# Expert weights loaded through two DMA queues: SyncE keeps the first, third and fifth pair, ACT takes the second, fourth and sixth

## The reference

```
for each expert e (its tokens xb):
    hgu   = xb @ w_up_gate[e] + b_up_gate[e]          # 1024 x 2048
    x_glu = min(hgu[:, :1024], 7);  x_lin = clip(hgu[:, 1024:], -7, 7)
    hact  = x_glu * sigmoid(1.702 * x_glu) * (x_lin + 1)
    y     = hact @ w_down[e] + b_down[e]              # 1024 x 1024
```

## Time and profile before

| | |
|---|---|
| median of three runs | 1576.78 us |
| profiled execution | 1576.77 us, span 1575.0 us |
| PE busy in the span | 1464.4 us (93%) |
| DVE, ACT, POOL busy | 465.3, 423.3, 458.0 us (30%, 27%, 29%) |
| SP's DMA queue (q1) | 498.71 MB, 78.7% of the 16 engines' time |
| ACT's DMA queue (q10) | 2.36 MB, 0.5% |
| mean granted PE clock | 0.981 |

### The profile page before, as it was taken

One profiled execution on the slowest core, in us unless ns is written; L12 is line 12 of the kernel. 1 busy time (PEld: TensorE's weight loads), 2 busy tenths in 40 slices (PEclk: granted clock), 3 DMA queues, 4 the chain that ended last, 5 costly groups with the idle time before them and its releaser, 6 DMA issues.

```text
span 1575.0 us, 18643 instructions
## 1 busy us (share of the span) xinstructions
PE 1464.4 (93%) x7492; PEld 828.8 (53%) x7493; DVE 465.3 (30%) x842; ACT 423.3 (27%) x564; POOL 458.0 (29%) x356
## 2 busy tenths in 40 slices
PE   8999999998898998899998898988899999999998
PEld 7887533333333333333333333333698767799986
DVE  6526411111111111111111111111557494323211
ACT  6354301101001001001001001001754775443332
POOL 6836000000000000000000000000779656689994
PEclk9999999999999999999999999999999999999999
DMA  9534899999999999999999999999655323545540
GB/s 344 203 111 148 364 427 427 429 425 428 425 427 428 427 427 427 426 427 427 427 429 426 426 426 428 426 429 402 203 176 178 129 87 132 189 134 187 188 161 27
DMA packets 93479, 502.32 MB, mean 319 GB/s; under 512 B 8091, under 2 KB 38419, under 8 KB 66643
## 3 DMA queue, kind: packets, MB, share of 16 engines
q1 hardware_dynamic: 91904, 498.71, 78.7%
q10 hardware_dynamic: 1491, 2.36, 0.5%
HBM read 500.00 MB, written 1.05 MB: 318 GB/s over the span
## 4 chain that ended last, share of the span: by engine, by line
PE 61%; DMA 26%; DVE 5%; ACT 4%; issue 2%; POOL 2%; SPq 0%; DVEq 0%; ACTq 0%
DMA ring<-in_w_up_gate 24%; PE PS L939 19%; PE PS L573 9%; PE PS L575 9%; PE PS L574 9%; PE PS L957 8%; POOL w_low L2413 2%; PE PS L900 1%; DMA ring<-in_w_ple_gate 1%; PE PS L946 1%; ACT w_high L1335 1%; DVE arena L2053 1%; DVE arena L2050 1%; DVE arena L2048 1%; ACT arena L1493 1%
## 5 line engine op out<-in xcount | busy, mean ns | idle before, releaser
L2413 POOL TENSOR_TENSOR w_low<-ring,w_high 128x512 fp32r<-128x512 f32 (+1 forms) x352 | 457.8, 1342 | 1095.8 <-ACT w_high L1335 1094.8
L939 PE MATMUL PS<-ring,arena 128*64 128x512 f32 x1792 | 408.1, 609 | 20.4 <-DMA ring<-in_w_up_gate 20.4
L939 PEld LDWEIGHTS PS<-ring,arena 128*64 128x64 f32 x1792 | 126.8, 140 | 284.3 <-issue 246.0
L957 PE MATMUL PS<-ring,arena 128*64 128x512 f32 x1024 | 238.5, 620 | 27.9 <-ACT arena L1493 27.9
L1484 ACT ACTIVATE arena<-arena 128x512 f32<-128x512 f32 x32 | 20.1, 630 | 761.6 <-DVE arena L2047 761.6
L1335 ACT ACTIVATE w_high<-ring 128x2048 fp32r<-128x2048 f32 (+1 forms) x89 | 166.3, 1880 | 112.4 <-PE PS L575 89.6
L957 PEld LDWEIGHTS PS<-ring,arena 128*64 128x64 f32 x1024 | 75.8, 142 | 168.5 <-issue 168.5
L2047 DVE TENSOR_SCALAR arena<-PS 128x512 f32<-128x512 f32 x32 | 22.1, 692 | 461.1 <-PE PS L939 461.1
L573 PE MATMUL PS<-w_high,XNT_h 128*128 128x512 f32 (+1 forms) x336 | 135.3, 403 | 3.9 <-DVE XNT_l L1763 2.2
L573 PE MATMUL PS<-XNT_h,w_high 128*128 128x256 f32 (+1 forms) x464 | 131.2, 283 | 2.2 <-DVE XNT_l L1746 1.3
L574 PE MATMUL PS<-w_low,XNT_h 128*128 128x512 f32 (+1 forms) x336 | 131.5, 391 | 0.0
(11 more groups left out here) (374 smaller groups left out, 1492.7 us busy)
## 6 DMA issues: line engine op xcount, KB each, us to landing
ring<-in_w_up_gate SPq DMA_DIRECT2D x112, 2048.0 KB, 23.0
ring<-in_w_down SPq DMA_DIRECT2D x64, 2048.0 KB, 21.4
ring<-in_w_in SPq DMA_DIRECT2D x35, 1024.0 KB, 5.5
ring<-in_w_gate_up SPq DMA_DIRECT2D x22, 1024.0 KB, 5.1
arena<-in_w_up_gate SPq DMA_DIRECT2D x16, 1024.0 KB, 20.9
cst<-in_w_up_gate SPq DMA_DIRECT2D x16, 1024.0 KB, 24.9
ring<-in_w_down SPq DMA_DIRECT2D x11, 1024.0 KB, 4.9
ring<-in_w_out SPq DMA_DIRECT2D x8, 1024.0 KB, 5.1
```

The costliest lines, as they stand in the source:

```text
L939: ins = nc.tensor.matmul(PS[64 * (n % 2):64 * (n % 2) + 64, 4 + n // 2, :], x, w[:, n * 512:(n + 1) * 512], start=False, stop=c == KC - 1, ...
L957: ins = nc.tensor.matmul(PS[64 * n:64 * n + 64, 7, :], lhs, w[:, k, n * 512:(n + 1) * 512], start=(j, k) == (0, 0), stop=(j, k) == (1, 3))
L2413: ins = nc.gpsimd.tensor_tensor(LOW[raw_slot(key)][:, at], slot(raw_slot(key))[:, at], HIGH[m % BUF][:, at].bitcast(F32), ALU.subtract)
```

## The change

The list `ON_SP` = (0, 2, 4) replaces the range of six in SP's `next_loads` and in the single expert between its two loops, so SP issues pairs 0, 2 and 4 of experts 1 to 31. Pairs 1, 3 and 5 are issued by ACT inside its expert loop: `next_pair(e, j)` waits until PE has used pair j of expert e and then issues pair j of expert e+1. The load of pair 1 stands ahead of the sigmoid, that of pair 3 behind the sigmoid and ahead of the spread copy, that of pair 5 behind the activation's copy. ACT's loop covers 31 experts, and expert 31 follows without loads. Expert 0 is still loaded by SP alone. The conditions of the waits, the slots, the sources and the sizes are as before.

```
+ON_SP = (0, 2, 4)
...
             def next_loads(i, first, early):
-                for j in range(PER_EXPERT):
+                for j in ON_SP:
...
-            for j in range(PER_EXPERT):
+            for j in ON_SP:
                 if j != TWICE:
                     sp.wait_ge(sem("w_used"), (IN_ORDER - 1) * PER_EXPERT + (before_experts + j + 1))
                     expert_load(IN_ORDER, j)
...
-            with act.Fori(0, E) as e:
+            def next_pair(e, j):
+                act.wait_ge(sem("w_used"), e * PER_EXPERT + (before_experts + j + 1))
+                src = (w_up[1:] if j < UPS else w_down_e[1:])[e]
+                rows = src[j * 256:(j + 1) * 256, :] if j < UPS else src[(j - UPS) * 512:(j - UPS + 1) * 512, :]
+                act.dma_start(slots2(EXPERT_SLOT[j]), rows.rearrange("(p k) n -> p (k n)", p=P)).then_inc(landed[EXPERT_SLOT[j]], 16)
+            def expert_copies(e, loads):
+                if loads:
+                    next_pair(e, 1)
                 sigmoid("glu", "sig", e + 1)
+                if loads:
+                    next_pair(e, 3)
                 act.wait_ge(sem("spread"), e + 1)
                 nc.scalar.activation(SPT, PS[:, 7, 0:256], ACT.Copy).then_inc(sem("sT_slots"), 1)
                 act.wait_ge(sem("hT_ps"), e + 1)
                 nc.scalar.activation(HTS, PS[:, 6, :], ACT.Copy).then_inc(sem("hT"), 1)
+                if loads:
+                    next_pair(e, 5)
+            with act.Fori(0, E - 1) as e:
+                expert_copies(e, True)
+            expert_copies(E - 1, False)
```

## The result

Over 12 runs each, the changed kernel took 1584.84 us (1579.05 to 1589.12), the kernel before 1576.88 us (1572.92 to 1578.47): a ratio of 1.0056, 95% interval 1.0047 to 1.0066. The medians differ by 8.0 us; the ratio goes by the means, which differ by 8.9. The profiled execution took 1583.52 us, 6.75 more than that of before.

A forecast was written before the change was run, and what follows sets the result against it. It took the DMA engines as the limit, 29.47 us an expert against PE's 27.20. Issues cost nothing; landing order delays the last down part 5.2 us, less 1.3 absorbed: 1576.77 plus 3.9 gives 1580.7 us, range 1570 to 1588.

The forecast's parts named there:

- if PE waits for pairs 0, 1 or 4: Sign in the profile after: PE waiting for loads of these pairs would show the prediction wrong.
- the waits at pair 3: Sign in the profile after: PE's waits on loads again at pair 3, about 2.2 us each.
- ACT's landings above 24 us: Sign in the profile after: ACT's pairs take a median above 24 us to land, its queue being at half rate.
- Where the time goes: Expert layer: DMA engines set the pace, 29.47 us an expert at 427 GB/s; PE needs 27.20, 2.27 less.
- Equal shares: DMA engines with two queues: a pair takes 9.82 us while the other queue has work, total rate as before.
- The rival of turns by whole pairs: Engines alternate queues by whole pairs, landing 4.91 us apart in the old order; 1576.8 us, nothing lost; chance 0.20.
- Two queues move more: Rival: filled gaps between one queue's loads raise the rate 0.9%, to 431 GB/s, giving 1572.8 us; chance 0.15.
- streams disturb each other: Rival: two interleaved streams lower the rate up to 1.4%, to 421 GB/s, giving 1587 to 1592.7 us; chance 0.12.
- ACT's issues cost nothing: ACT's expert loop: three more issues an expert, 0.33 to 0.68 us each, fit into its idle time; cost nothing.
- The step that failed: Steady pace: only ACT's pair 3 late, by 2.27 us; SP's pair 4, landing a later, never delays PE.
- The term that was mis-sized: Last expert's down part: one-time delay of (9.8 - a) / 2, 5.2 us at a = -0.6; 7.6 and 2.9 at the ends.
- What reaches the end: After the expert layer: of 5.2 us, PE's 1.3 us wait for POOL takes up part, and 3.9 us stay.

The follow-up runs named there:

- columns_two: Kernel before, each load cut into first and last 2048 columns, SP issuing one half and ACT the other, both in the old order: 1589.18 us, ratio 1.0079.
- columns_sp: Kernel before, each load cut into first and last 2048 columns, both halves issued by SP: 1589.24 us, ratio 1.0082.
- all_on_act: Kernel before, with ACT issuing all loads of experts 1 to 31 in the old order and SP none: 1576.31 us, ratio 1.0005.
- swapped: Changed kernel with the pairs exchanged, SP issuing 1, 3, 5 and ACT 0, 2, 4: 1588.4 us, ratio 1.0084.
- near_two: Changed kernel with pair 2 loaded a whole expert ahead for the first three experts only, not for 21: 1587.72 us, ratio 1.0073.
- halves_two: Kernel before, each load cut into partitions 0 to 63, issued by SP, and 64 to 127, issued by ACT, in the old order: 2271.47 us, ratio 1.4416.
- halves_sp: Kernel before, each load cut into partitions 0 to 63 and 64 to 127, both issued by SP: six runs from 2272.07 to 2384.68 us, no ratio given.

## Why the prediction was right in its direction, and where it failed

Forecast 1580.7, measured 1584.84; the range held, and the sign with its reason, the order of landing. The size was half of what was measured, and the late loads were others than I had said. By the prediction's own list of signs, "if PE waits for pairs 0, 1 or 4", its path to the number was wrong, and two more of its signs failed: the waits at pair 3 and ACT's landings above 24 us. That the time still fell into the range is in part luck: the range was wide enough for the rivals.

- *Where the time goes* was right: 29.47 us an expert for the DMA engines, 27.20 for PE, and nothing in the change that touches the one or the other. 427 and 426 GB/s say that the pace stayed.
- *Equal shares* was right for rows, and so for bytes only while the rows are alike: 50.3% and 49.9%, but 65.9% and 35.3% while SP's queue is in rows of 8 KB. The prediction did not reckon with these. The rival of turns by whole pairs is out. It would land pairs in the old order, with waits at pair 3 alone; instead pairs of one stream land after 15.4 us and those of the other after 21.5, and an engine changes queue from row to row in most steps. The Trainium skill ("DMA: Bandwidth & Descriptors", Queues, rings and completion order) has the engine go round its queues by whole packets; by that rule the rival held only if an engine's whole part of a pair were one packet. The landings and the turns by single rows show that it isn't served as one.
- *Two queues move more* and *streams disturb each other* are out by the same rates, and the latter by columns_two against columns_sp as well. A few slices in the changed kernel are lower (406, 422, 424), which was not expected. They come where PE has stood for some us and freed no place: from 727.2 us, behind the wait of 6.84 for a load, the rate is 391 for 6.2 us (below); from 880 to 885 us, behind a loop's turn of 3.34, it is 377. They don't make the last data later (1096.6 in both kernels), so they are no part of the cost.
- *ACT's issues cost nothing* was right: 0.34 us each, the spread copy behind them still waits 0.92 us for PE, as in the earlier trace rows; and all_on_act.
- *The step that failed* is the one that kept pair 3, on ACT, as the load that PE waits for, with SP's queue at some a between -5.3 and 4.1 us of it that "holds PE back nowhere". The runs show the other branch: SP's pairs bind, pair 4 above all, and PE waits for none of ACT's, which land after 15.4 us where I had expected over 24. I had set up the steady pace from the landing of ACT's pair 3, as if PE had waited for it, and then asked whether SP fits beside it; from this came "so ACT's queue never runs dry". It does, for 47 us in all. A stream that is ready early has no reason to fall back, and the other catches up only while the first is empty. Both branches keep the pace of 29.47, so the pace told nothing about which it would be.
- *The term that was mis-sized*: (9.8 - a) / 2 = 5.2 us, for bytes moved beside what PE needs at the last pair 3; measured 7.1 at the last `down`. Its a, the time of SP's pair 4 against that pair 3, has no counterpart in the branch that came. There the size is PE's delay against the kernel before at its last wait, 9.8 us at pair 2 of expert 29, less the 2.7 that it makes up until the last `down`. The lower clock behind that wait, 3.3 us, stood in no term.
- *What reaches the end*: I had 1.3 us absorbed at POOL's splits, and so 3.9 left of 5.2. Measured, the wait there fell only from 1.3 to 0.9, so 6.7 of 7.1 stayed, which is the difference of the spans (1581.7 less 1575.0):

```profile
PE PS L574 <- POOL w_low L2432: 0.9, 1, 0.9
```

ACT's splits stood ready without a wait for their piece, as forecast: behind the last copy they run back to back.

```profile
1101.27 0.60 ACT L1506 ACTIVATE arena<-PS 128x512 f32<-128x512 f32 x1 [0.99 <-PE PS L947]
1101.84 7.40 ACT L1336 ACTIVATE w_high<-ring 128x2048 fp32r<-128x2048 f32 x4
```

*What stays open.* Why the stream 0, 2, 4 falls behind and not 1, 3, 5. It goes with the pairs, not the queue (swapped). The traces point to the rows of 8 KB: once in two experts this stream moves the 256 rows of an odd pair 2, 2 MB, while the other moves as many rows of 16 KB, 4 MB, two pairs for one. The runs swapped and near_two hold the same rows in the same stream; in columns_two all rows are alike on both queues, and PE is not behind the data. No run gave an odd pair 2 rows of 16 KB, so this is argued, not shown, and pair 2's second place remains a rival. That PE would free 1, 3 and 5 more evenly explains little: ACT issued them 7.7, 10.9 and 8.6 us apart in an early expert of the changed kernel, SP its own 6.9, 11.7 and 8.6. Nor is it settled why PE ends 8.5 and 8.2 us behind the data in swapped and near_two, and 5.5 in the change.

## What to carry to other kernels

When a consumer takes large transfers in a fixed order and the DMA engines are the limit, one queue that holds that order is worth more than two: two queues move the same bytes per us, but part of the engines' time goes to whichever stream is ahead, row against row, and the queue with the shorter rows gets the smaller share. If two queues must be used, cut each transfer by columns over both, in the same order, rather than dealing out whole transfers. Here that cost nothing against the same cut in one queue, though the shorter rows themselves cost 1.4% of the rate; no run had two queues with neither cost. In a profile, compare the time from issue to landing by queue: where one is far under the time at which its place is needed and the consumer waits for the other, bytes are moving in the wrong order, even though no rate and no busy share has changed.

## What the runs showed of the hardware that was not expected

- Loads that cover 64 partitions moved 251 GB/s on two queues and 247 on one, against 427 for the same bytes over 128 partitions, with the DMA engines shown as busy throughout (halves_two, halves_sp). The Trainium skill ("SBUF — State Buffer", "Can I just issue two DMAs to hit both halves?") says that two transfers to the two halves of the partitions gain hardly anything over one, from whichever engines they are issued. These two runs agree on the issuing engines: 251 GB/s from two and 247 from one, the fastest executions 2263.29 and 2272.07 us. What one half gives without the other no run shows.
- Two filled queues share the engines row by row, not byte by byte: 107 and 107 packets, 1.67 and 0.89 MB, from 642 to 648 us of the changed kernel.
- Rows of 8 KB for a partition instead of 16 KB: 421 against 427 GB/s, 1.4% (columns_two, columns_sp).
- Behind a long wait PE is slower for a while. Before the down part at 723.72 us in the changed kernel PE stood almost still for 7 us; then (length, busy us by engine, granted clock, DMA share, GB/s):

```profile
716.80:723.80 7.00, 0.16 (x3) 0.09 (x4) 0.00 (x0) 0.60 (x1) 0.00 (x0) 0.64 1.01 428
723.80:727.20 3.40, 3.40 (x10) 0.93 (x12) 0.00 (x0) 0.00 (x0) 0.00 (x0) 0.50 1.01 429
727.20:733.40 6.20, 6.20 (x27) 1.85 (x23) 0.00 (x0) 0.00 (x0) 0.00 (x0) 0.86 0.97 391
```

The granted clock is 0.50 (1.2 GHz) for 3.4 us, 0.86 in the mean of the next 6.2, and the part takes 9.68 us instead of 7.09. In the sum this makes no difference here: the matmuls on the ring are busy for 646.2 us in all, and were for 646.6, since before has such stretches behind its own waits. At the end of the layer it does, where no wait follows that could take it up (the 3.3 us above).
